# Routed experts: rows weighed on ScalarE and summed in memory by accumulating indirect transfers

## The chip, the core and the metric

One core of a Trainium2 chip (trn2) runs the whole program. The metric is the device time of one execution in microseconds. Engines: PE is TensorE, DVE VectorE, ACT ScalarE, POOL GpSimd, SP SyncE. Everything is fp32 unless a type is named.

## The reference

Two transformer blocks on 512 tokens of 1024 values. The change touches only the last stage, a mixture of experts in which each token goes to 4 of 32 experts:

```
logits = hf @ w_router + b_router
top_val, top_idx = top_k(logits, 4); gates = softmax(top_val)
# per expert e, over the tokens that chose it:
gu = xb @ w1[e] + b1[e]                       # 1024 -> 2048
gate, up = min(gu[:, :1024], 7), clip(gu[:, 1024:], -7, 7)
act = (up + 1) * gate * sigmoid(1.702 * gate)
y = (act @ w2[e] + b2[e]) * g[:, None]        # g: the pair's gate
out[tok] += y                                  # 4 addends per token
return rmsnorm(x + out, g_final)
```

Before it come a mixer, a first block with a product-key memory (512 gathers of rows of 8 KB) and a second block's attention and memory attention.

## The kernel before, in words

All engines' programs are written out by hand, in blocks; semaphores order them. The blocks before the experts take 1889 us. The middle part (`mid_sp`, L1301, loads its weights) ends with `store_rows`, which writes the normed token rows to `moe_dram` for the experts. `h` holds the residual, four tiles of 128 tokens.

*Positions.* Experts are sorted by their number of tokens; position p has a capacity of 128 rows (p 0 to 2), 96 (3 to 15, and 31) or 64 (the rest), by `capacity`. `ORDER` runs position 31 first, then alternates one of the wide positions with a 64-row one, then 15 and 30. A position has a first part of 64 rows and, if it is wider, a second part of 32 or 64 (`parts`). Tokens that are beyond the capacity would go to extra blocks of 64 rows, whose number is a register value (`each_extra`); the trace shows none.

*Weights.* An expert has six chunks of 2 MB (`expert_w`): four for gate and up, two for down. They go through a ring of nine slots. SP issues each load when PE has used the slot's last chunk (L2681, and L2710 for the last expert). Chunk number 8 lands on the tables from which the routing lists are made, so its load waits for `pe["slots2"]` and `dve["gk"]`.

*One expert.* POOL gathers its token rows (`rows_of`, L2725). PE transposes them (L2815), multiplies (gate and up: `into`, L2829; down: `out_of`, L2841; biases L2847), and transposes the activation (`transpose_act`, L2822). DVE clips (L3032), multiplies (L3037) and activates (`activate`, L3046 and L3048). ACT does sigmoid (L2965), copies (L2969) and, in `store` (L2974), copies the product from PSUM to `ysb`, which is the same memory as `usb`; then it issues the stores into `y_dram` (L2979), by position and row. `activate` writes `usb` again, so it first waits for the stores of the expert before (`y_st`). An fp32 product is four passes in the trace, so one call shows as four instructions.

*Routing lists.* During the first expert, DVE makes one-hot tables: `rowhot` (row in its position) and `poshot` (position), the same again for extra blocks. PE multiplies them into `slots` (L2805) and `slots2` (L2878), lists of the token in each row. Then DVE works out where each pair's row will lie in `y_dram` (`srow`, L3194 to L3203), the extra blocks' experts and the gates `gk` (L3204 to L3216).

*Fills.* Rows of `y_dram` that no expert writes are read by gathers all the same in some cases, so 37 stores fill them from SBUF during the middle part (L1360, L1366).

*End.* During the last expert POOL gathers, for each of 16 pairs (4 tiles by 4 choices), 128 rows from `y_dram` into weight slots that came free (`rows_back`, L2752), 12 at a time; DVE adds each to `h` times its gate (`add`, L3270). Two additions stand in DVE's order before the last expert's clip and three more before its activation. The rows of the last expert but one and of the last come in two rounds of four gathers (`add_late`, L3276). Then ACT squares and takes the root (L3013, L3016), DVE scales (L3284), SP stores.

Of the kernel before, what the change touches and what calls it, by code (L numbers as in the profile page):

```python
# [47 lines left out]
NBO = 32  # L48
BATCH = 32
# [17 lines left out]
for _name, _w in (("ident", P), ("lt", P), ("gt", P), ("ones", P), ("bones", P), ("wsmask", P),  # L67
                  ("iota", P), ("tok", NT), ("emod", P), ("rev", NE), ("rcount", 4 * PADU), ("zero", P), ("eps", 2)):
    _C[_name] = (_n, _w)
    _n += _w  # L70
# [13 lines left out]
def constants():  # L84
# [20 lines left out]
    put("eps", np.array([[EPS1, EPS2]]))  # L105
    return c
# [16 lines left out]
def build(nc, t, out):  # L123
    ctx = ExitStack()
    with ctx:
# [33 lines left out]
        y_dram = nc.dram_tensor("expert_rows", (OVER_AT + NBO * 64, D), F32).ap()  # L159


        last_dram = nc.dram_tensor("last_expert_rows", (64, D), F32).ap()
        prev_dram = nc.dram_tensor("last_but_one_expert_rows", (capacity(ORDER[-2]), D), F32).ap()
# [7 lines left out]
        rows_filled = sem("rows_filled")  # L171
# [1138 lines left out]
        def mid_sp(sp):  # L1310
# [17 lines left out]
            for j, unit in enumerate(unit_order):  # L1328
# [27 lines left out]
                if unit == ("o2", LAST, 3):  # L1356
                    fills = 0
                    any_rows = region(8192, 2 * D).rearrange("p (t d) -> p t d", t=2)
                    for i in range(OVER_AT, OVER_AT + NBO * 64, W):
                        sp.dma_start(y_dram[i:i + W, :].rearrange("(t p) d -> p t d", p=P), any_rows).then_inc(rows_filled, 16)  # L1360
                        fills += 1
                    by_position = y_dram[0:OVER_AT, :].rearrange("(q r) d -> r q d", r=P)
                    for cap, positions in ((64, range(16, NE - 1)), (96, list(range(3, 16)) + [NE - 1])):
                        for q in positions:
                            filled_from = 0 if q in ORDER[-2:] else cap
                            sp.dma_start(by_position[filled_from:P, q, :], any_rows[0:P - filled_from, q % 2, :]).then_inc(rows_filled, 16)  # L1366
                            fills += 1
# [10 lines left out]
            sp.wait_ge(rows_filled, 16 * fills)  # L1378
# [1160 lines left out]
        srow = small(16, NPAIR, I32)  # L2539
# [6 lines left out]
        lastm, rowf, lpart, glast, gk_rest, either = (small(1920 + i * NPAIR, NPAIR) for i in range(6))  # L2546
        erow = small(1920 + 6 * NPAIR, NPAIR, I32)
        prevm = small(227, NPAIR)
        lsum = small(243, NT)
        gl = [small(247 + i * NT, NT) for i in range(2)]  # L2550
        lrow = [small(255 + i * NT, NT, I32) for i in range(2)]
# [3 lines left out]
        before_last = sb("before_last", [P, 2], I32)  # L2555
        hot2 = sb("hot2", [3 * NE, 64], BF16)
        curs = sb("curs", [64, 1], I32)

# [9 lines left out]
        PIECE = NC // 2  # L2568

# [7 lines left out]
        def stored_rest(upto):  # L2577
            return sum(16 * P // x[1][1] for x in parts[0:upto] if len(x) > 1)

# [3 lines left out]
        pool_turn = sem("pool_turn")  # L2583
        x_t = sem("x_t")
# [13 lines left out]
        y_st = [sem(f"y_st{i}") for i in range(2)]  # L2598
        pe_turn = sem("pe_turn")

# [13 lines left out]
        NOWHERE = 2 * OVER_AT  # L2614
        Y_ROWS = OVER_AT + NBO * 64
        assert capacity(LAST_AT) == 64
        got = [slot(placed(FINAL - 1, c))[:, j * D:(j + 1) * D] for c in (3, 4, 5) for j in range(4)]
        late = [slot(placed(FINAL, 0))[:, j * D:(j + 1) * D] for j in range(NT)]
        prev = [slot(placed(FINAL, 2))[:, j * D:(j + 1) * D] for j in range(NT)]
        result = [slot(placed(FINAL, 1))[:, j * D:(j + 1) * D] for j in range(NT)]  # L2620
        NGOT = len(got)
        got_in = [sem(f"got_in{j}") for j in range(NGOT)]
        late_rows_in = [sem(f"late_rows_in{j}") for j in range(NT)]
        prev_rows_in = [sem(f"prev_rows_in{j}") for j in range(NT)]
# [8 lines left out]
        dvl += ["selr", "rsel", "selp", "psel", ("cap1", 0), ("cap2", 0), ("cap3", 0), ("cap4", 0), "beyond", "lastm", "prevm", "rowa", "rowhot", "poseq", "poshot"]  # L2633
        dvl += ["slots"]
        dvl += [("cap1", 1), ("cap2", 1), ("cap3", 1), ("cap4", 1), "spare", "spare64", "oge", "nb2", "bend2", "bst2", "live2", "any2", "turned2", "turn2", "stored2", "selb", "b2sel", "r2",
                "r64", "qge", "q2", "row2", "blk2s", "rowhot2", "blkeq", "blkhot2", "slots2", "base1", "base2", "gap", "gap2", "frow", "srow",
                "cmpb", "blk2f", "blk2m", "blk2", "esum", "erec", "gk", "rowf", "either", "erow", "grest", "gk_rest"]
        dvl += [(x, i) for i in range(2) for x in ("lpart", "lsum", "lrow", "glast", "gl")]
        dv = steps("dve", dvl)
        ac = steps("act", ["exp"])  # L2640
        BEFORE_CLIP, BEFORE_ACT = 2, 5
        end_dv = steps("dve", [("add", tt, k) for tt in range(NT) for k in range(EK)] + [("prev", tt) for tt in range(NT)]
                       + [x for tt in range(NT) for x in [("last", tt)] + ([("rstd", tt - 1), ("scale", tt - 1)] if tt else [])]
                       + [("rstd", NT - 1), ("scale", NT - 1)])
# [3 lines left out]
        pe = steps("pe", ["lgT", "lg", "cnt", "rank", "slots0", "slots", "slots2"])  # L2648
# [17 lines left out]
        with nc.Block() as block:  # L2666
            @block.sync
            def _(sp):
                def load(s, c, e6):
# [36 lines left out]
                for c in range(6):  # L2706
# [13 lines left out]
            def _(eng):  # L2720
# [14 lines left out]
                eng.wait_ge(dve_done, dv["slots2"])  # L2735

                def body(b):
# [7 lines left out]
                       .then_inc(rows_in, 16)  # L2745
                n = each_extra(eng, body)
# [3 lines left out]

                def rows_back(dst, src, nrows, index, sem_):
                    eng.indirect_dma_start(dst, None, src, bass.IndirectOffsetOnAxis(ap=index, axis=0),  # L2752
                                           bounds_check=nrows - 1, oob_is_err=False)\
                       .then_inc(sem_, 16)

                eng.wait_ge(dve_done, dv["gl", 1])
                eng.wait_ge(y_st[1], stored_rest(FINAL - 1))
                eng.wait_ge(y_st[0], eng.value_load(before_last[0:1, 1:2], min_val=32 * (FINAL - 1), max_val=32 * (FINAL + NOVER)))
                eng.sem_inc(pool_turn, 1)
                for i in range(NPAIR):  # L2760
                    if i < NGOT and i % 4 == 0:
                        eng.wait_ge(w_used[3 + i // 4], FINAL)
# [597 lines left out]
```

## Time and profile before

| | us |
|---|---|
| median of 3 runs (2967.68 to 2970.21) | 2967.72 |
| profiled execution | 2963.5 |
| its span | 2961.7 |
| PE busy in the span | 2394.2 (81%) |
| DVE busy | 1403.1 (47%) |
| ACT busy | 867.5 (29%) |
| POOL busy | 736.2 (25%) |
| data moved | 1098.90 MB, 371 GB/s on average |

Busy shares are averages over stages with different limits; the chain of waits says what the end hung on. From 1906 us on the program is in its expert stage. DMA shares are shares of the time of all 16 engines. A matmul that waits in the queue is drawn longer than it works, so a busy share alone doesn't show that PE sets the pace.

### The profile page before, as it was taken

Reading aid. Unit: us, or ns where it says so; the run is one execution under the profiler, and the core shown is the slowest. Engines: PE = TensorE matmul, PEld = TensorE weight load, DVE = VectorE, ACT = ScalarE, POOL = GpSimd, SP = SyncE. Lnnn points to the kernel's source line nnn. Section 1 sums busy time; section 2 is a strip of 40 time slices with the busy share of each in tenths; the row PEclk is TensorE's granted clock in tenths of the full one; section 3 lists DMA queues with packets and bytes.
Section 4 is the critical chain, followed back from the end, with each engine's and each line's share of the span. In section 5 each row is a group of like instructions: output and inputs, shape, how many; then the busy total and the mean of one; then the engine's idle time right before and its main releaser. Section 6 shows DMA issues by size and latency. Waiting matters only on the chain. (4 is left out here: it accounts for less than half of the span.)

```text
span 2961.7 us, 35151 instructions
## 1 busy us (share of the span) xinstructions
PE 2394.2 (81%) x13231; PEld 1140.0 (38%) x13231; DVE 1403.1 (47%) x3100; ACT 867.5 (29%) x2616; POOL 736.2 (25%) x663
## 2 busy tenths in 40 slices
PE   8998896675435695566678998699999999999995
PEld 4444442242001362124345787433333333333332
DVE  3967776767778766654655433531111111111115
ACT  1133334544445546522632341101000101001001
POOL 0313444433444445542643011100000000000003
PEclk9999998786656897587888999899999999999998
DMA  4349999999999999999999667899999999999996
GB/s 180 112 150 377 410 398 393 421 415 418 418 420 391 408 412 399 409 411 415 414 421 410 265 235 218 320 386 407 420 414 405 420 414 405 413 421 406 414 415 261
DMA packets 151243, 1098.90 MB, mean 371 GB/s; under 512 B 19616, under 2 KB 27040, under 8 KB 51648
## 3 DMA queue, kind: packets, MB, share of 16 engines
q0 software_dynamic: 80384, 553.69, 46.0%
q1 hardware_dynamic: 62112, 531.15, 44.8%
q10 hardware_dynamic: 8576, 11.80, 1.1%
q8 instruction: 105, 1.72, 0.2%
q14 instruction: 66, 0.54, 0.0%
HBM read 1071.80 MB, written 31.59 MB: 373 GB/s over the span
## 5 line engine op out<-in xcount | busy, mean ns | idle before, releaser
L2428 PE MATMUL banks<-arena,spare 128*32 128x512 f32 (+1 forms) x2048 | 484.1, 787 | 419.1 <-ACT spare L2290 412.6
L2061 POOL DMA_INDIRECT arena<-in_expert_uv,picked x512 | 584.7, 1142 | 870.8 <-PE banks L2428 619.1
L2196 DVE SCALAR_TENSOR_TENSOR arena<-arena 128x1024 f32<-128x1024 f32 x384 | 472.9, 1234 | 345.7 <-DMA arena<-in_expert_uv,picked 345.2
L2829 PE MATMUL banks<-arena,aT 128*64 128x512 f32 (+1 forms) x4032 | 616.1, 506 | 22.4 <-DMA arena<-in_expert_w 17.7
L2829 PEld LDWEIGHTS banks<-arena,aT 128*64 128x64 f32 (+1 forms) x4032 | 215.7, 126 | 396.4 <-issue 352.2
L2428 PEld LDWEIGHTS banks<-arena,spare 128*32 128x32 f32 (+1 forms) x2048 | 84.1, 132 | 710.4 <-ACT spare L2290 581.1
L3032 DVE TENSOR_SCALAR aT<-banks 128x512 f32<-128x512 f32 (+1 forms) x49 | 30.0, 614 | 593.3 <-PE banks L2847 593.3
L2841 PE MATMUL banks<-arena,aT 128*64 128x512 f32 (+1 forms) x2016 | 304.5, 502 | 0.3 <-DMA arena<-in_expert_w 0.3
L2725 POOL DMA_INDIRECT picked<-moe_rows,extra x32 | 31.0, 969 | 962.2 <-PE banks L2815 902.8
L2275 ACT ACTIVATE spare<-spare 128x2 f32<-128x2 f32 x256 | 51.9, 203 | 654.7 <-DVE arena L2196 654.1
L2196 DVE SCALAR_TENSOR_TENSOR arena<-arena,extra 128x1024 f32<-128x1024 f32 x128 | 156.5, 1224 | 89.3 <-DMA arena<-in_expert_uv,picked 89.1
L2841 PEld LDWEIGHTS banks<-arena,aT 128*64 128x64 f32 (+1 forms) x2016 | 103.9, 125 | 167.1 <-issue 146.6
L2969 ACT ACTIVATE aT<-banks 128x256 f32<-128x256 f32 x84 | 31.9, 383 | 382.0 <-PE banks L2822 382.0
L1294 PE MATMUL banks<-arena,aT 128*128 128x256 f32 x576 | 137.2, 395 | 0.0
L3046 DVE TENSOR_SCALAR aT<-banks 128x256 f32<-128x256 f32 x84 | 35.3, 420 | 214.5 <-PE banks L2847 214.5
L2290 ACT ACTIVATE spare<-spare 128x32 f32<-128x32 f32 (+1 forms) x512 | 136.3, 313 | 0.0
L2283 ACT ACTIVATE spare<-spare,picked 128x1 f32<-128x1 f32 x512 | 122.9, 287 | 11.7
L1294 PEld LDWEIGHTS banks<-arena,aT 128*128 128x128 f32 x576 | 111.0, 197 | 37.7 <-issue 20.1
L2965 ACT ACTIVATE aT<-aT 128x512 f32<-128x512 f32 (+1 forms) x49 | 27.8, 569 | 327.2 <-DVE aT L3032 327.2
L2390 PE MATMUL banks<-aT,arena 128*128 128x128 f32 (+1 forms) x512 | 122.0, 387 | 0.0
L1296 PE MATMUL banks<-aT,arena 128*128 128x256 f32 x448 | 107.1, 395 | 0.4 <-DVE aT L1258 0.4
L551 PE MATMUL banks<-aT,arena 128*128 128x512 f32 x240 | 103.4, 593 | 1.6 <-PEq L317 1.6
(368 smaller groups left out, 2715.5 us busy)
## 6 DMA issues: line engine op xcount, KB each, us to landing
arena<-in_expert_w SPq DMA_DIRECT2D x192, 2048.0 KB, 34.4
arena<-in_mid_w SPq DMA_DIRECT2D x71, 1024.0 KB, 9.1
expert_rows<-aT ACTq DMA_DIRECT2D x66, 128.0 KB, 9.2
arena<-in_w_q SPq DMA_DIRECT2D x4, 2048.0 KB, 11.1
arena<-in_expert_uv,picked POOLq DMA_INDIRECT x512, 12.6
expert_rows<-arena SPq DMA_DIRECT2D x8, 1024.0 KB, 14.5
arena<-in_w_in SPq DMA_DIRECT2D x3, 2048.0 KB, 13.7
arena<-in_w_out SPq DMA_DIRECT2D x2, 2048.0 KB, 7.8
```

Of the source, the lines that this page charges most:

```text
L551: mm = nc.tensor.matmul(bank[:, j % 8, :], w[:, k, col:col + P], aT[:, k, :], start=k == 0, stop=k == KD - 1)
L1294: mm = nc.tensor.matmul(dst, src[:, k, j * P:(j + 1) * P], w[:, k, :], start=k == 0, stop=k == KD - 1)
L1296: mm = nc.tensor.matmul(dst, w[:, k, j * P:(j + 1) * P], src[:, k, :], start=k == 0, stop=k == KD - 1)
L2061: eng.indirect_dma_start(places[place_of[n]], None, uv_rows, bass.IndirectOffsetOnAxis(ap=eidx[:, n:n + 1], axis=0))\
L2196: nc.vector.scalar_tensor_tensor(out=u, in0=u, scalar=1.0, in1=token_rows(tt)[:, g, :], op0=ALU.mult, op1=ALU.mult, accum_out=dots[:, k:k ...
L2275: nc.scalar.activation(gelus[:, k:k + PAIR], dots[:, k:k + PAIR], ACT.Gelu_apprx_tanh).then_inc(gelu_done, 1)
L2283: nc.scalar.activation(acts[:, k + i:k + i + 1], gelus[:, k + i:k + i + 1], ACT.Copy, scale=gates[:, n + i:n + i + 1]).then_inc(acts_done, 1)
L2290: nc.scalar.activation(diag[:, (n + i) % NDIAG, 0:width], ident4 if tt else ident2, ACT.Copy, scale=acts[:, k + i:k + i + 1]).then_inc(dia ...
L2390: mm = nc.tensor.matmul(bank[:, 4 + i % 2, t0 * P:t1 * P], w[:, k, g % 4 * P:(g % 4 + 1) * P], aT[:, k, t0 * P:t1 * P], start=k == 0, stop ...
L2428: mm = nc.tensor.matmul(bank[lo:lo + width, sum_bank[tt] + half, :], diag[:, (n + g) % NDIAG, 0:width], places[place_of[n + g]][:, D + hal ...
L2829: mm = nc.tensor.matmul(bank[tile, b_, 0:width], xT[:, c % 2 * 4 + k, r0:r0 + nrows], w[:, k * D + lo:k * D + lo + width], start=c % 2 == ...
L2841: mm = nc.tensor.matmul(bank[tile, YB[i], 0:width], hv[:, kk % nj, kk // nj * nrows:(kk // nj + 1) * nrows], w[:, k * D + lo:k * D + lo + ...
```

## The change

The gate is applied on ACT and the sum over a token's four experts is formed in memory. `sum_dram` (512 + 128 rows) starts as a copy of `h`. Each part of an expert goes to it in one indirect transfer on POOL's queue that adds: 128 partitions, each half a row (64-row parts) or a quarter (32-row parts). Row lists for it (`dest`) and gates by row (`gain`) are made from the one-hot tables; unused rows get an address past 512, one each. At the end SP reads `sum_dram` back into `h`. The fills, `y_dram`, the gathers back and DVE's additions go. Transfers that add wait for one another between experts.

In the middle part, SP:

```diff
-                if unit == ("o2", LAST, 3):
-                    ... 37 fills of y_dram
             for s in range(PASSES):
                 store_rows(s)
-            sp.wait_ge(rows_filled, 16 * fills)
+                if s != TOGETHER[0]:
+                    for tt in range(NT - 1) if s < LAST else (NT - 1, NT):
+                        rows_ = h[:, tt % NT, :]
+                        sp.dma_start(sum_dram[tt * P:(tt + 1) * P, :], rows_).then_inc(sum_begun, 16)
             sp.wait_ge(moe_rows_out, 64)
```

In the expert stage, SP, then POOL:

```diff
                     if i == 8:
-                        sp.wait_ge(pe_done, pe["slots2"])
-                        sp.wait_ge(dve_done, dv["gk"])
+                        sp.wait_ge(pe_done, pe["gains"])
...
+                sp.wait_ge(all_added, 16)
+                for tt in range(NT):
+                    sp.dma_start(h[:, tt, :], sum_dram[tt * P:(tt + 1) * P, :]).then_inc(sum_in[tt], 16)
```

```diff
+                def add_rows(i, nrows, index, landed):
+                    width = D * nrows // P
+                    eng.indirect_dma_start(halves_of_sum if nrows == 64 else quarters_of_sum, bass.IndirectOffsetOnAxis(ap=index, axis=0),
+                                           ysb[i][:, 0:width], None, compute_op=ALU.add)\
+                       .then_inc(landed, 16)
+
+                def add_first(s):
+                    eng.wait_ge(y_out[0], s + 1)
+                    if s:
+                        eng.wait_ge(y_added[0], 16 * s)
+                    after(eng, y_added[1], 16 * seconds[s])
+                    add_rows(0, 64, dest[0][:, ORDER[s]:ORDER[s] + 1], y_added[0])
+
+                def add_second(s):
+                    if len(parts[s]) > 1:
+                        eng.wait_ge(y_out[1], seconds[s] + 1)
+                        add_rows(1, parts[s][1][1], dest[1][:, ORDER[s]:ORDER[s] + 1], y_added[1])
                 for s, p in enumerate(ORDER[0:FINAL]):
...
                     rows_of(p)
+                    if s == 2:
+                        eng.wait_ge(sum_begun, 16 * (NT + 1))
+                        eng.wait_ge(dve_done, dv["gain", 1, 1])
+                    if s >= 2:
+                        add_first(s - 2)
+                        add_second(s - 2)
...
-                eng.wait_ge(y_st[0], n * 32 + (32 * FINAL + 32))
-                for tt in range(NT):
-                    rows_back(late[tt], last_dram, 64, lrow[1][:, tt:tt + 1], late_rows_in[tt])
+                add_second(FINAL - 1)
+                eng.wait_ge(y_added[1], 16 * seconds[FINAL])
+                eng.wait_ge(y_out[0], n + (FINAL + 1))
+                add_rows(0, 64, dest[0][:, LAST_AT:LAST_AT + 1], all_added)
```

PE: `gain_lists` stands in expert 0 between the transposes of the second part's activation and the down-projection's second chunk; `spread_lists` stands at the head of expert 1.

```diff
+                def gain_lists():
+                    eng.wait_ge(dve_done, dv["pair", 1, 3])
+                    for c in range(NPAIR):
+                        nc.tensor.matmul(lists[:, 0:3 * NE], rowhot[:, c, :], pairs[0][:, c, 1:4, :], start=c == 0, stop=c == NPAIR - 1)
+                    ... the same for the extra blocks
+                def spread_lists():
+                    eng.wait_ge(dve_done, dv["tlo", 1])
+                    for i, (x, lo, nrows, width) in enumerate(((0, 0, 64, 2 * NE), (0, 64, 32, 2 * NE), (0, 64, 64, 2 * NE), (1, 0, 64, 2 * NE))):
+                        for n in range(P // nrows):
+                            ... one product of 64 columns, from ident and table
```

ACT:

```diff
-                def store(i, nrows, nth, row, into=y_dram):
+                def weigh(i, nrows, nth, by):
                     width = D * nrows // P
                     eng.wait_ge(y_done[i], nth)
-                    nc.scalar.activation(ysb[i][:, 0:width], bank[:, YB[i], 0:width], ACT.Copy).then_inc(y_out[i], 1)
-                    eng.wait_ge(y_out[i], nth)
-                    for n in range(P // nrows):
-                        ... eng.dma_start(dst, ysb[i][...]).then_inc(y_st[i], 16)
+                    nc.scalar.activation(ysb[i][:, 0:width], bank[:, YB[i], 0:width], ACT.Copy, scale=by).then_inc(y_out[i], 1)
```

DVE: `srow` and `last_picks` go. After the first expert's `copy_rows` stand `which_blocks` (the former L3204 to L3216), `pair_gains` (gates split in three fp16 parts, then six products of 128x512 with the one-hot tables), `slot_gains` and `slot_lists` (small operations). Four small operations on `table` stand ahead of the first activation. `activate` waits for `y_added[i]` where it waited for `y_st[i]`. At the end only the scaling is left:

```diff
-                for i in range(BEFORE_CLIP):
-                    add(i)
                 clip_gate(0, 64, n + (FINAL + 1))
                 gated(0, 64, n + (FINAL + 1))
-                for i in range(BEFORE_CLIP, BEFORE_ACT):
-                    add(i)
                 activate(...)
-                for i in range(BEFORE_ACT, NPAIR):
-                    add(i)
-                ... add_late for the last two experts
                 for tt in range(NT):
-                    ...
+                    scale(tt)
```

## Rows read from the trace of the kernel before

**Rows 1.** Windows: stretch, length, busy (instructions) by engine, PEclk, DMA share, GB/s

```profile
2700.00:2800.00 100.00, 99.48 (x784) 38.37 (x782) 13.13 (x29) 9.87 (x22) 2.87 (x3) 1.00 1.01 407
```

**Rows 2.** Chain of waits, 1959 to 2843 us: start, duration, what

```profile
1959.56 9.03 PE banks L2829 x64
...
2018.60 9.03 PE banks L2829 x64
...
2205.22 9.03 PE banks L2829 x64
...
2334.63 40.87 DMA arena<-in_expert_w
...
2842.19 9.03 PE banks L2829 x64
```

**Rows 3.** DMA queues and issues, 2000 to 2600 us: packets, MB, share; landing last

```profile
q1 hardware_dynamic: 16158, 235.38, 95.1%
q10 hardware_dynamic: 4704, 6.43, 2.9%
q0 software_dynamic: 1872, 5.09, 2.6%
...
expert_rows<-aT ACTq DMA_DIRECT2D x42, 128.0 KB, 9.2
```

**Rows 4.** PE's waits, 1750 to 1890 us: total us, times, longest

```profile
PE banks L1294 <- DMA arena<-in_mid_w: 0.4, 1, 0.4
```

**Rows 5.** Windows, end of the middle part

```profile
1880.00:1885.00 5.00, 2.25 (x11) 1.64 (x9) 1.14 (x3) 1.44 (x3) 0.00 (x0) 1.00 0.23 91
```

**Rows 6.** Timeline of the first expert: start, duration, what, [idle before]

```profile
1922.18 0.56 PE L2805 MATMUL banks<-arena 128*128 128x32 f16 x16
...
1932.29 0.69 DVE L3189 TENSOR_TENSOR arena<-arena,cst 128x512 f16<-128x512 f16 x1
...
1938.15 1.22 DVE L3204 TENSOR_TENSOR arena<-arena,cst 128x1024 f32<-128x1024 f32 x1
...
1940.76 3.65 PE L2841 MATMUL banks<-arena,aT 128*64 128x512 f32 x16
...
1942.12 0.34 SPq L2681 DMA_DIRECT2D arena<-in_expert_w  x1
```

**Rows 7.** Landings of L2681's loads issued 1888 to 1890, then at 1982.13

```profile
DMA to landing us min/median/max: 7.7/12.2/16.6
...
DMA to landing us min/median/max: 10.3/10.3/10.3
```

**Rows 8.** Chain of waits, 1975 to 2002 us

```profile
1979.84 0.22 PE banks L2847 x2
...
1998.12 0.44 DVE aT L3046
```

**Rows 9.** Timeline of the last expert and the tail

```profile
2921.59 0.38 PE L2847 MATMUL banks<-spare,hot 96*64 96x512 bf16 x1
...
2923.93 1.28 DVE L3270 SCALAR_TENSOR_TENSOR h<-arena,extra,h 128x1024 f32<-128x1024 f32 x1 [3.51 <-DMA arena<-expert_rows,extra]
...
2927.51 8.05 PE L2841 MATMUL banks<-arena,aT 128*64 128x512 f32 x32
...
2935.83 0.60 ACT L2974 ACTIVATE aT<-banks 128x512 f32<-128x512 f32 x1 [7.82 <-PE banks L2847]
...
2955.64 1.06 ACT L3013 ACTIVATE arena<-h 128x1024 f32<-128x1024 f32 x1 [1.11 <-DVE h L3276]
...
2957.35 1.28 DVE L3284 SCALAR_TENSOR_TENSOR arena<-h,stat,grow 128x1024 f32<-128x1024 f32 x1
```

**Rows 10.** DMA issues of the whole span: times, KB each, median us to landing

```profile
arena<-expert_rows,extra POOLq DMA_INDIRECT x16, 23.0
...
arena<-last_expert_rows,extra POOLq DMA_INDIRECT x4, 3.1
```

More of the change, by code:

```diff
@@ L105, in constants @@
     put("eps", np.array([[EPS1, EPS2]]))
+    put("row", p)
+    put("half", p // 64)
+    put("quarter", p // 32)
     return c
@@ L2538, in build @@
         gk = small(0, NPAIR)
-        srow = small(16, NPAIR, I32)
+        gsplit = [small(16 + i * NPAIR // 2, NPAIR // 2, F16) for i in range(2)] + [small(227, NPAIR // 2, F16)]
+        grest = small(235, NPAIR)
         posf = small(32, NE)
@@ L2545, in build @@
         slots2 = small(194, NBO + 1, I32, 64)
[L2546 to L2551, printed above, removed]
+        table = [small(1920, 2 * NE), small(1920 + 2 * NE, 2 * NE, rows_=64)]
+        dest, gain = ([small(lo + i * NE, NE, dt) for i in range(2)] for lo, dt in ((1408, I32), (1408 + 2 * NE, F32)))
+        dest2, gain2 = small(1408 + 4 * NE, NBO + 1, I32), small(1408 + 5 * NE + 1, NBO)
+        pairs = [grow[:, :].bitcast(F16).rearrange("p (c j e) -> p c j e", c=NPAIR, j=4),
+                 extra[:, 384:384 + D].bitcast(F16).rearrange("p (c j e) -> p c j e", c=NPAIR, j=4)]
         any2 = small(263, 1)
@@ L2583, in build @@
         pool_turn = sem("pool_turn")
+        dest_copied = sem("dest_copied")
+        gain_copied = sem("gain_copied")
+        all_added = sem("all_added")
+        sum_in = [sem(f"sum_in{i}") for i in range(NT)]
         x_t = sem("x_t")
@@ L2597, in build @@
         y_out = [sem(f"y_out{i}") for i in range(2)]
-        y_st = [sem(f"y_st{i}") for i in range(2)]
+        y_added = [sem(f"y_added{i}") for i in range(2)]
         pe_turn = sem("pe_turn")
+        act_turn = sem("act_turn")
         def slot(i):
@@ L2639, in build @@
+        dvl += [("pair", x, j) for x in range(2) for j in range(1, 4)]
+        dvl += [(name, x) for x in range(2) for name in ("filled", "row", "thi", "tmid", "tlo")]
+        dvl += [("dest", 0), ("gain", 0), ("dest2",), ("gain2",), ("dest", 1, 0), ("dest", 1, 1), ("gain", 1, 0), ("gain", 1, 1)]
         dv = steps("dve", dvl)
         ac = steps("act", ["exp"])
[L2641 to L2644, printed above, removed]
+        end_dv = steps("dve", [x for tt in range(NT) for x in (("rstd", tt), ("scale", tt))])
@@ L2901, in _ @@
                             transpose_act(1, q)
+                    if s == 0:
+                        after(eng, h_e[1], pieces[1])
+                        gain_lists()
                     eng.wait_ge(w_loaded[placed(s, 5)], loads(s, 5))
@@ L2991, in _, with block_of_64 @@
                             copy_act(1, q, pieces[s] + q + 1)
-                    for i, (r0, nrows) in enumerate(parts[s]):
-                        if s == FINAL - 1:
-                            store(i, nrows, nth[i], r0, prev_dram)
-                        else:
-                            store(i, nrows, nth[i], p * P + r0)
-                def block_of_64(before, row, into, more):
+                    if s == 0:
+                        eng.wait_ge(dve_done, dv["gain", 1, 1])
+                    for i, (_, nrows) in enumerate(parts[s]):
+                        weigh(i, nrows, nth[i], gain[i][:, p:p + 1])
+                def block_of_64(before, more):
                     sigmoid(0, 64, before + (FINAL + 1))
@@ new lines, in slot_lists, with destinations, gains @@
+                def slot_lists():
+                    eng.wait_ge(pe_done, pe["spread"])
+                    def destinations(out_, i, n, times, place):
+                        V(nc.vector.scalar_tensor_tensor(out=out_, in0=lists[:, i * 2 * NE + n.start:i * 2 * NE + n.stop], scalar=times,
+                                                         in1=const(place).to_broadcast([P, n.stop - n.start]), op0=ALU.mult, op1=ALU.add))
+                    def gains(out_, i, n):
+                        V(nc.vector.tensor_copy(out_, lists[:, (2 * i + 1) * NE + n.start:(2 * i + 1) * NE + n.stop]))
+                    destinations(dest[0], 0, slice(0, NE), 2.0, "half")
+                    gains(gain[0], 0, slice(0, NE))
+                    destinations(dest2[:, 1:NBO + 1], 3, slice(0, NBO), 2.0, "half")
+                    gains(gain2, 3, slice(0, NBO))
+                    wide = next(p for p in range(NE) if capacity(p) < P)
+                    destinations(dest[1][:, 0:wide], 2, slice(0, wide), 2.0, "half")
+                    destinations(dest[1][:, wide:NE], 1, slice(wide, NE), 4.0, "quarter")
+                    gains(gain[1][:, 0:wide], 2, slice(0, wide))
+                    gains(gain[1][:, wide:NE], 1, slice(wide, NE))
```

274 lines of the change are left out of this document (130 added, 144 removed).

## The prediction

> **What bounds the kernel now.** I first took the windows view of the expert stage (from about 1909 us to the end). Over 2700 to 2800 us TensorE is busy 99.48 of 100 us and the sixteen DMA engines are busy all the time, at 407 GB/s [rows 1]. Both look full, so the next question is which of them sets the pace. The chain of waits answers it. The same point of the loop (up-projection of a 96-row expert) stands at 1959.56 and at 2018.60 us, so an undisturbed pair of a 96-row and a 64-row expert takes 59.04 us. From 2018.60 to 2205.22 us two such pairs and one of 128 and 64 rows take 186.62 us, so the long pair takes 68.54 us. Between 1959.56 and 2842.19 us lie 11 short pairs and 3 long ones: 11 x 59.04 + 3 x 68.54 = 855.1 us of TensorE work. They took 882.6 us. The other 27.5 us are waits for expert weights, as in the piece at 2334.63 us, where the chain runs through a weight load for 40.87 us [rows 2]. TensorE alone would need 27.5 us less. The rate of the DMA engines sets the end of this stage, although TensorE shows 99%: a matmul that waits for a weight tile is drawn long.
>
> So every byte moved in this stage counts, and it is the price of bytes that I look for. From 2000 to 2600 us the weights (q1) take 95.1% of the engines' time, the stores of expert rows (q10) 2.9%, the indirect gathers of token rows (q0) 2.6% [rows 3].
>
> After the last expert's down-projection the trace shows a tail: 2935.83 us (its copy out of PSUM) to the span's end at 2961.7 us. The profiled run took 2963.5 us, 1.8 more than its span.
>
> **The change, part by part.**
>
> *Fills removed.* 37 stores issued between 1754 and 1805 us go. In that stretch and up to 1890 us TensorE waited for its middle weights 0.4 us in all [rows 4]; its other waits are on VectorE. The cover is TensorE's own work, and nothing is late behind them. Gain between 0 and 0.4 us: 0.
>
> *Sum rows begun.* SyncE now stores token rows of `h` before the block ends: three tiles of 512 KB ahead of the last `moe_rows` store, two more behind it, ahead of expert weights 3 to 5. The queue is nearly empty then (the engines are busy 23% of 1880 to 1885 us [rows 5]). The three (1.57 MB, 3.8 us at 412 GB/s) could hold the block's end by 0 to 3.8 us, two more issues on SyncE cost their own fractions. I take 0.7, near the low end because of that idle time. The last two (1 MB) go into a queue that is refilled only after the expert numbers are known: hidden.
>
> *Lists for gates and destinations.* This is inside expert 0. VectorE today computes from 1938.15 us on what becomes `which_blocks`, up to `gk`, after which SyncE issues the held load of weight chunk 8 at 1942.12 us. Now `pair_gains` follows: six dependent small operations (about 0.2 each, 1.3 us) and six of 128x512 at 0.69 us (4.1), so the pairs are ready at about 1947.0 us. TensorE stands at `gain_lists` in its order, ahead of the down-projection that today starts at 1940.76 us. Its 32 small matmuls, three times as wide as the 16 that take 0.56 us, cost 1.1 to 3.4, say 1.6 us: it resumes at about 1948.6. With 0.4 us of list operations in front of the activation, that is 8.3 us of delay. `spread_lists` at the start of expert 1 adds 10 fp32 products in four passes of 64 columns, 40 instructions; a 512-column one takes 228 ns, so the bounds are 0.06 to 0.23 each, 2.4 to 9 us; I take 3.7, since the columns are few. Together TensorE is 12.0 us late [rows 6].
>
> What of this reaches the end? Only what starves the DMA engines, since they are the bound. Chunk 8 and all loads that wait for a used slot are issued that much later. The load issued at 1982.13 us landed after 10.3 us, and the first of an empty queue after 7.7 [rows 7], so only 2.6 us of work was queued before it. Twelve us later issue leaves 12.0 - 2.6 = 9.4 us in which the engines idle. Bounds: 5 (if only chunk 8's hold counts) to 12.
>
> *Stores become accumulating transfers.* Each expert now sends all its capacity rows (unused ones to rows past 512). Capacities sum to 2688 rows; without the last three experts 2432 rows, 9.96 MB, fall where the engines bind. A store reads SBUF and writes memory. An accumulate must also read the destination row. The trace before has no such transfer. From below: it costs no more than the store it replaces, 0 us, or even less (a store takes 2.9% of 882.6 us = 25.6 us in all; half of that gone is -12). From above: four times a store, +77. I take one more load of the same bytes on top of the store, since reading rows is what is added: 9.96 MB at 412 GB/s, +24 us. By the gathers' own rate (5.09 MB in 2.6%, so 6.43 MB of stores would be 3.3%) it would be +29 [rows 3].
>
> The Trainium skill (DMA: Bandwidth & Descriptors, Rules for kernel authors) states that the accumulate reads its destination and writes it later, and that nothing holds the bytes in between, so each must wait for the semaphore of the one before. By that the second read is there and the sum keeps its +24; without it the sum would be 24 lower. No run here shows it yet.
>
> *The new waits.* On GpSimd `add_first` waits for the copy out of PSUM, for the expert before, and for its predecessor's second part; queued behind it is the gather of rows two experts on, which is needed only some 30 us later. On VectorE `activate` waits for `y_added`, and TensorE's transposes wait for it. From the end of the 96-row expert's first part at 1980.06 us to the next activation at 1998.12 us lie 18.1 us [rows 8]. Minus 0.6 for the weighing and 0.8 for GpSimd to start, a landing may take 16.7 us. Stores land in 9.2 us at the median [rows 3]. I take 12 to 15: covered, no cost.
>
> *ScalarE's weighing* is the same copy with a scale, 0.60 us: 0. Its DMA issues go; it was never late.
>
> *Last expert.* Today VectorE stands in an addition that waited for a gather until 2923.93 us and ended at 2925.2, while the up-projection's last matmul had ended at 2922.0 [rows 9]. These 3.1 us go, and about 1.0 more, since TensorE's down-projection ran slower after its idle time (32 matmuls in 8.05 us, against 16 in 3.65 [rows 6, 9]). Late next is nothing: the weights have landed. -4.1, bounds -5 to 0.
>
> *Tail.* New chain from the copy's start: weigh 0.6, GpSimd 0.8, one accumulate on an empty queue. The gathers there land in 3.1 us [rows 10]; half the bytes, but with a second access, 4.0. Then four loads of 512 KB: the first lands after 3.1 like those gathers of the same size, and ScalarE is late next: four tiles of square (1.06 + 0.19) and root (0.29) with one table load 1.28, 4 x 1.65 + 1.3 = 7.9, then reciprocal and scale 1.5, and from the end of the last scaling the 3.1 that the span has today. 0.6 + 0.8 + 4.0 + 3.1 + 7.9 + 1.5 + 3.1 = 21.0, against 25.9 from 2935.83 to 2961.7 [rows 9]: -4.9, bounds -8 to +1.
>
> By the fit that the skill gives (same page, Anatomy of one DMA: 2.0 us fixed plus bytes at 436 GB/s) this accumulate of 256 KB would land in 2.6 us and the sum would be 1.4 lower.
>
> **Sum:** 0.7 + 9.4 + 24 - 4.1 - 4.9 = +25.1, so 2963.5 + 25.1 = 2988.6 us by the profiled execution. The median of the runs is 4.2 above that execution, so I forecast 2992.8, say 2993 us.
>
> **Rivals.**
> A. *Accumulate priced as a store.* If the second access overlaps the first, +24 becomes 0: sum +1.1, about 2969 us; a little cheaper than a store (-12) gives 2957. For it: the engines are held most by weights written into SBUF, and this traffic only reads SBUF. Against: stores do take time in proportion to their bytes. 0.22.
> B. *The DMA engines stop being the bound* (mechanism on the faster side): accumulates and the gone ACT queue leave the weights' stream so much room that TensorE never waits. Then the stage is 27.5 us shorter and pays the full 12.7 of start: -27.5 + 12.7 - 9.0 = -23.8, 2944 us. Against: stores take 25.6 us in all, so they would have to be nearly free. 0.06.
> C. *The landing holds VectorE* (slower side). It decides from 16.7 us of landing. The sixteen gathers at the end landed in 23.0 us at the median on the same queue [rows 10]. At 23, each turn from 96 to 64 rows loses 6.3 and the turn back 1.0: 15 x 7.3 = 110 us, TensorE bound: -27.5 + 12.7 + 110 - 9.0 = +86, 3054 us. 0.10.
> Forecast: 0.62.
>
> **How the numbers follow.** The forecast's own range is 2975 to 3015. 2955 to 3028 leaves out B, the far end of A and most of C: under 0.2. About 0.2% (5.9 us) is what a measurement can tell from no change: 2961.8 to 2973.6. Faster: B 0.06 and 0.08 of A with 0.02 of the forecast, 0.16. Same: 0.13 of A and 0.05 of the forecast, 0.18. Slower: 0.66.
>
> **What would show it.** Right: TensorE idle for some 6 us at about 1941 us and the loop 12 us late at 1960; q0 with far more engine time per MB than q10 had; longer DMA waits in the chain between 2200 and 2830 us; the pair still 59 us where it doesn't wait; tail about 21 us. Wrong: the distance from 1959.56 to 2842.19 unchanged or shorter (A, B); VectorE L3046 waiting for DMA in each pair (C); an accumulate that lands in over 6 us on an empty queue.

## The result, and the profile after

| us | before | after |
|---|---|---|
| median of the runs beside each other (5 and 5) | 2967.68 | 2994.32 (2989.43 to 3003.95) |
| ratio, 95% interval | | 1.0097 (1.0082 to 1.0112) |
| profiled execution, span | 2963.5, 2961.7 | 3003.95, 3002.0 |

The change makes the kernel slower by 26.6 us at the medians (24 to 33 us by the interval of the ratio). The forecast was 2993. The profiled execution of the kernel after is the slowest of its runs, and it was already 7.7 us late at the start of the middle part, in code that the change doesn't touch. So I compare distances between fixed points of each trace, not its times: from the first router product to the first up-projection of expert 1 (start), on to that of expert 29 (loop), on to the last copy out of PSUM (end), and to the end of the span (tail).

| us | start | loop | end | tail | sum |
|---|---|---|---|---|---|
| before | 70.7 | 882.6 | 93.6 | 25.9 | 1072.8 |
| after | 83.9 | 907.8 | 90.8 | 22.1 | 1104.7 |
| difference | +13.2 | +25.2 | -2.8 | -3.7 | +31.9 |

Three kernels that have the same code up to expert 29 (after, and two of the experiments) take 991.8, 988.6 and 987.2 us for start and loop together, so one profile can't tell 2 us of it.

The page after, part 1 and the end of part 3. There are fewer bytes than before (1098.90 MB), and yet it takes longer.

```profile
PE 2400.9 (80%) x13283; PEld 1140.1 (38%) x13283; DVE 1379.6 (46%) x3086; ACT 872.2 (29%) x2616; POOL 794.6 (26%) x690
DMA packets 143643, 1080.42 MB, mean 360 GB/s; under 512 B 16528, under 2 KB 23952, under 8 KB 44048
HBM read 1061.31 MB, written 19.40 MB: 360 GB/s over the span
```

**The start.** The timeline of the kernel after, expert 0, the counterpart of [rows 6] (start, duration, engine, line; in brackets the idle time before it and what ended it). Lines 2858, 2870 and 2876 are the gate and up projections, the down-projection and the biases; 2844 and 2851 the transposes of token rows and of the activation; 3265 and 2822 `pair_gains` and `gain_lists`; 3079 the activation; 3010 and 2721 the weighing and the accumulate.

```profile
1948.24 3.65 PE L2870 MATMUL banks<-arena,aT 128*64 128x512 f32 x16
1953.68 1.90 DVE L3265 TENSOR_TENSOR grow<-arena,extra 128x512 f16<-128x512 f16 x3
1955.49 1.89 DVE L3265 TENSOR_TENSOR extra<-arena,extra 128x512 f16<-128x512 f16 x3
1957.53 1.44 PE L2822 MATMUL banks<-grow,arena 128*128 128x96 f16 x16 [5.27 <-DVE extra L3265]
1960.03 0.41 PEld L2870 LDWEIGHTS banks<-arena,aT 128*64 128x64 f32 x4
```

TensorE is idle for 5.27 us (some 6 forecast) and then works on the lists; its next down-projection stands at 1960.03, after one at 1948.24. Before, the two chunks followed each other without such a hole (3.96 us apart). The windows view of the same moment shows why this counts: columns are the busy time of PE, PEld, DVE, ACT and POOL, then the granted clock, the DMA share and GB/s. The first two rows are the kernel after, the other two the kernel before at the same distance from the router product.

```profile
1952.27:1957.27 5.00, 0.00 (x0) 0.00 (x0) 4.76 (x13) 0.39 (x1) 0.00 (x0) 0.85 0.17 39
1957.27:1962.27 5.00, 4.74 (x38) 3.49 (x40) 1.72 (x10) 0.00 (x0) 0.00 (x0) 0.50 0.28 52
```

```profile
1943.89:1948.89 5.00, 5.00 (x78) 2.48 (x76) 0.00 (x0) 0.98 (x2) 0.00 (x0) 1.00 0.95 374
1948.89:1953.89 5.00, 5.00 (x50) 1.84 (x46) 0.00 (x0) 0.00 (x0) 0.00 (x0) 1.00 0.98 400
```

The DMA engines move 39 and 52 GB/s where they moved 374 and 400. The granted clock also falls to 0.50, 1.2 GHz, after the engine's idle stretch. In the first 140 us after the router product the DMA engines idle for 15.0 us, 5.0 before: 10.0 more, where 9.4 was forecast. Four experiments with the same lists (`plain`, `skip`, `order`, `fills`) idle for 15.6, 15.0, 13.1 and 13.1 us, so this number is known to some 2 us.

**The loop.** The DMA queues of the kernel after from 2000 to 2600 us, the counterpart of [rows 3] (packets, MB, share of 16 engines; then issues and the median us to landing).

```profile
q1 hardware_dynamic: 15593, 227.06, 92.0%
q0 software_dynamic: 6050, 11.67, 8.8%
summed_rows<-aT,extra POOLq DMA_INDIRECT x29, 12.1
```

q0 now holds the gathers of token rows, 2.6% before, and the accumulates: 6.2% of the time for 6.6 MB, 5.7 us of all engines per MB. The stores that they replace took 2.9% for 6.43 MB, 2.7 us per MB. The weights get 92.0% where they had 95.1%. The chain of waits of the kernel after, the counterpart of [rows 2]:

```profile
1981.19 9.03 PE banks L2858 x64
...
2040.23 9.03 PE banks L2858 x64
...
2238.19 38.23 DMA arena<-in_expert_w
...
2829.23 45.38 DMA arena<-in_expert_w
...
2889.03 9.03 PE banks L2858 x64
...
2913.01 0.48 ACT aT L3010
...
2913.76 14.64 DMA summed_rows<-aT,extra
...
2930.90 8.80 DMA picked<-moe_rows,extra
```

Where it doesn't wait, a pair still takes 59.04 us (2040.23 - 1981.19). So the 25 us of the loop are waits for weights and no work. The waits of TensorE and of VectorE (us in total, times, longest) say the same, and rule rival C out: VectorE's line 3079 waits for TensorE, never for an accumulate. The first row is the kernel before; between the same points of the kernel after the waits for weights are twice as long. The last row of TensorE holds two waits for gathers of token rows. The one of 8.9 us is that of the first expert, which took 8.0 before; the other, 4.3 us, was in no forecast.

```profile
PE banks L2829 <- DMA arena<-in_expert_w: 17.7, 9, 3.8
```

```profile
PE banks L2858 <- DMA arena<-in_expert_w: 36.2, 18, 3.4
PE banks L2844 <- DMA picked<-moe_rows,extra: 13.2, 2, 8.9
```

```profile
DVE aT L3079 <- PE banks L2876: 234.8, 47, 10.6
```

**The end.** The timeline of the kernel after around that 4.3 us wait, GpSimd and then TensorE:

```profile
2913.76 1.55 POOL L2721 DMA_INDIRECT summed_rows<-aT,extra  x1 [1.93 <-ACT aT L3010]
2928.45 0.19 POOL L2752 COPY extra<-extra 128x1 int32<-128x1 int32 x1 [13.15 <-DMA summed_rows<-aT,extra]
2930.90 1.02 POOL L2715 DMA_INDIRECT picked<-moe_rows,extra  x1 [2.26 <-issue]
...
2939.74 0.69 PE L2844 MATMUL banks<-cst,picked 64*128 64x64 f32 x4 [4.33 <-DMA picked<-moe_rows,extra]
...
2942.21 5.34 PE L2870 MATMUL banks<-arena,aT 128*64 128x512 f32 x16
```

GpSimd waits 13.15 us for an accumulate to land, to protect the order of the sums, and the gather of the last expert's token rows stands behind that wait in its queue. TensorE's transposes of these rows (L2844) wait 4.33 us for it, and the products behind them are slower: sixteen take 5.34 us, where 3.65 is usual (the granted clock is 0.50 during the transposes and 0.68 during the sixteen products). In the tail, the last accumulate (2982.30 us) lands after 4.9 us, and ScalarE's first square starts at 2990.45.

### The profile page after: what moved, and what is told of

It reads as the page before. It is cut to its first block and busy times, and to the rows that moved or that the text cites. A ratio compares the mean times of both kernels' runs of the same rounds, so it can differ in the third digit from the quotient of the medians.

```text
span 3002.0 us, 35101 instructions
## 1 busy us (share of the span) xinstructions
PE 2400.9 (80%) x13283; PEld 1140.1 (38%) x13283; DVE 1379.6 (46%) x3086; ACT 872.2 (29%) x2616; POOL 794.6 (26%) x690
## 3 DMA queue, kind: packets, MB, share of 16 engines
HBM read 1061.31 MB, written 19.40 MB: 360 GB/s over the span
## 5 line engine op out<-in xcount | busy, mean ns | idle before, releaser
L2721 POOL DMA_INDIRECT summed_rows<-aT,extra x49 | 76.7, 1565 | 328.0 <-ACT aT L3010 301.6
L1297 PEld LDWEIGHTS banks<-arena,aT 128*128 128x128 f32 x576 | 111.6, 198 | 38.0 <-issue 20.1
```

The source lines that it names most:

```text
L1297: mm = nc.tensor.matmul(dst, src[:, k, j * P:(j + 1) * P], w[:, k, :], start=k == 0, stop=k == KD - 1)
L2721: eng.indirect_dma_start(halves_of_sum if nrows == 64 else quarters_of_sum, bass.IndirectOffsetOnAxis(ap=index, axis=0), ysb[i][:, 0:width ...
```

## Experiments

The edits are against the kernel after, unless said otherwise. Ratios are to the kernel before, run beside each experiment on the same chip: in 5 rounds for `best`, `turn`, `best_mid` and `best_early`, in 3 for the others. The chips differ from one group of experiments to the next (the medians of the kernel before are 2963.3 to 2967.7 us), so compare ratios and distances, not the times themselves. "Sum" is the last column of the table above.

**plain.** Is it the adding that costs, or the transfer? The transfer writes over its rows, so the sum isn't formed.

```diff
-    ysb[i][:, 0:width], None, compute_op=ALU.add)\
+    ysb[i][:, 0:width], None)\
```

> The changed kernel with the same indirect transfers on the same queue, but plain stores without the addition (the sum is not formed, so its result is wrong at will; all waits stay). Theory: what the accumulate costs is its second access, the read of the destination rows, in engine time. Then q0's share between 2000 and 2600 us falls from 8.8% to 5.5%, the distance from expert 1's up-projection to expert 29's (907.8 us) falls by 25 to 30, and the time by about 27, to 2967 us. Rival: the engine time comes from the indirect path and its small packets, not from the addition: share and distance stay, 2994 us.

2959.51 us, ratio 0.9988 (0.9979 to 0.9998). Loop 881.9, end 83.9, tail 19.1, sum 1068.7: 36.0 below the kernel after. Its queues:

```profile
q0 software_dynamic: 3936, 11.65, 5.3%
...
summed_rows<-aT,extra POOLq DMA_INDIRECT x28, 7.1
```

The same bytes take 3.5% of the engines' time less and land 5 us sooner. The loop is 25.9 us shorter, which is all that the change had added to it (25.2). What remains of the transfers' engine time, 2.7%, is about what the stores took (2.9%). Rival A (the second access costs nothing) falls. The same bytes show as fewer, larger packets here (3936 against 6050 in q0), but small packets aren't the reason: in the kernel after an accumulate's packet of 2 KB takes 181 ns on average, and a store's packet of 2 KB in the kernel before took 85. That the extra time is the read of the destination isn't shown: the page counts 1061.31 MB read from HBM in both kernels. The end is 6.9 us and the tail 3.0 us shorter as well, which wasn't expected: GpSimd's wait at the end is 6.7 us instead of 13.15.

**narrow.** The same number of accumulates with an eighth or a quarter of the bytes each (64 columns; the rest of the rows isn't added).

```diff
-    halves_of_sum = ...("r (c d) -> (r c) d", c=2)
-    quarters_of_sum = ...("r (c d) -> (r c) d", c=4)
+    both with c=16
-    ysb[i][:, 0:width], None, compute_op=ALU.add)\
+    ysb[i][:, 0:64], None, compute_op=ALU.add)\
```

> The changed kernel with accumulating transfers of 64 values per partition instead of 512 or 256 (the rest of the sum is left out); their number, partitions, waits and queue stay. Theory (bytes on the DMA engines): q0 falls to 3 to 4.5% between 2000 and 2600 us, the distance between expert 1 and expert 29 falls from 907.8 by 38 or more, to 855 to 870, TensorE's own floor being 855; time about 2950 us. Rival (waiting for landings or the number of transfers holds the loop): the distance stays above 895.

2952.58 us, ratio 0.9963 (0.9954 to 0.9973). Loop 869.0, q0 4.3%. The end stays at 90.7 us. So the loop's cost goes mainly by bytes (a seventh of them takes 1.7% of the engines' time, where all took 6.2%) and the end's by the wait: the small accumulates still land in 10.9 us at the median, and GpSimd still waits 12.0 us for one at the end.

**skip.** Rows that no token fills are dropped instead of added past row 512.

```diff
-    ysb[i][:, 0:width], None, compute_op=ALU.add)\
+    ysb[i][:, 0:width], None, bounds_check=S * P // nrows - 1, oob_is_err=False, compute_op=ALU.add)\
```

> The changed kernel, but unused capacity rows (640 of 2688, 24%) are skipped by a bound on the destination index, as the gathers already do. If engine time goes by rows that move: 24% of 6.3% of 883 us = 13 us less, about 2981 us. Rival: a skipped descriptor costs as much as a moved one: 2994 us.

2983.22 us, ratio 1.0067 (1.0050 to 1.0084). Loop 895.4, that is 12.5 less. Its queue:

```profile
q0 software_dynamic: 6048, 10.42, 7.6%
```

The dropped rows go on showing as packets (6048 against 6050), but neither as bytes nor as engine time. About half of what the loop had lost was spent on rows that nobody reads. In the kernel before, those rows were stored too.

**later.** The lists wait until TensorE has finished expert 0's down-projection; the second list stands behind the first weight chunk of expert 1.

```diff
-                    if s == 1:
-                        spread_lists()
...
+                        if s == 1 and c == 0:
+                            spread_lists()
...
-                    if s == 0:
-                        gain_lists()
...                     # both chunks of the down-projection
+                    if s == 0:
+                        gain_lists()
```

> The changed kernel with gain_lists behind the whole down-projection of expert 0 and spread_lists behind the first chunk of expert 1; the held load of chunk 8 still waits for gain_lists. TensorE then resumes about 8 us earlier. Theory (the start's delay counts only as far as it starves the DMA engines; my 9.4 us were 12.0 minus 2.6 of queued work): the hold of chunk 8 (5.7 us) stays, so the end comes 3 to 4 us earlier. Rival (TensorE's delay reaches the end in full): 8 us earlier.

2988.45 us, ratio 1.0085 (1.0067 to 1.0104). The start is 6.6 us shorter than the kernel after's (4.4 and 4.0 shorter than those of `order` and `fills`, 81.7 and 81.3), but start and loop together are only 2.8 below the mean of the three kernels with the original order (989.2), about their own scatter. The DMA engines' idle time in the first 140 us, 13.6, lies among the 13.1 to 15.6 of the kernels with the original order: chunk 8 is now issued 65.4 us after the router product instead of 63.3 (61.4 to 63.3 in the same-code kernels), since it waits for the lists. So what TensorE gained at the start didn't reach the end in full. What did reach it is within the noise, and even its sign isn't settled by these runs.

**order.** The wait that holds GpSimd moves behind the last expert's gather.

```diff
-                eng.wait_ge(y_added[1], 16 * seconds[FINAL - 1])
                 eng.tensor_copy(dest2[:, 0:1], ...)
                 ... the gather of the last expert's rows
+                    eng.wait_ge(y_added[1], 16 * seconds[FINAL - 1])
```

> The changed kernel with GpSimd's wait for the second part of expert 29's accumulate moved behind the gather of the last expert's rows. Theory: that gather was issued at 2930.90 us, 14.6 us of landing too late, which cost TensorE 4.3 us of idle time at 2939.74 and some 2 us of lower granted clock. Both go: the time from the last chunk-c=2 piece of expert 29 to the span's end falls by 5 to 7 us. Rival: the last expert's weights would have been late anyway: 0 to 1 us.

2986.08 us, ratio 1.0074 (1.0057 to 1.0091). The end is 83.87 us instead of 90.84: 7.0 less. GpSimd in this kernel:

```profile
2901.82 1.55 POOL L2721 DMA_INDIRECT summed_rows<-aT,extra  x1 [1.93 <-ACT aT L3010]
2903.42 0.19 POOL L2751 COPY extra<-extra 128x1 int32<-128x1 int32 x1
2905.94 1.02 POOL L2715 DMA_INDIRECT picked<-moe_rows,extra  x1 [2.33 <-issue]
```

The gather now follows the accumulate by 4.1 us, where it was 17.1. TensorE's transposes start right behind the product before them, and the sixteen products behind take 3.65 us again: 4.3 us of idle time and 2.6 of slower products (1.7 here, 0.9 in the transposes) make the 7.0. So the place of this wait costs 7.0 us.

**fills.** The 37 stores of the kernel before are put back in the middle part, into rows that nobody reads.

```diff
+                if unit == ("o2", LAST, 3):
+                    ... the 37 fills of the kernel before
+            sp.wait_ge(rows_filled, 16 * fills)
```

> The changed kernel with the 37 fill stores of the middle part put back (into rows that nothing reads). Theory: TensorE's own work covers them: 0 us (within 1), the stretch from 1750 us to the first router product unchanged at 147 us. Rival: they held weights of the middle part or the block's end: 3 us or more slower.

2990.83 us, ratio 1.0085 (1.0067 to 1.0102). The middle stretch takes 146.9 us with the fills, 147.1 without, 146.5 in the kernel before; the sum is 1102.0 and 1104.7. Removing them gave nothing.

**best.** skip, later and order together, and VectorE computes the extra blocks' table behind `pair_gains` instead of ahead of it, while TensorE makes the lists; chunk 8 waits for both.

> The changed kernel with unused rows skipped, lists later, GpSimd's wait moved, and the experts-of-blocks table computed while VectorE waits. Sum of the single expectations: 13 + 4 + 6 + 1 = 24 us less than the changed kernel, about 2970 us, which is the time of the kernel before (2967.7) within its spread. If skipped rows cost as much as moved ones: 2983 us.

2972.44 us, ratio 1.0028 (1.0018 to 1.0038): still slower than before. Start 74.5, loop 898.7, end 83.9, tail 22.4, 1079.5 in all. The loop still has 16 us more than before: q0 takes 7.5% of the engines' time from 2000 to 2600 us, where stores and gathers took 5.5% before.

**turn.** In the kernel before, VectorE adds one gathered tile less ahead of the last activation. That is the edit that asks whether the forecast's two gains at the end are two.

```diff
-        BEFORE_CLIP, BEFORE_ACT = 2, 5
+        BEFORE_CLIP, BEFORE_ACT = 2, 4
```

> The kernel before with one addition moved from before the last expert's activation to after it (BEFORE_ACT 4 instead of 5). My forecast took 3.1 + 1.0 us for this wait. If it was on the path alone: TensorE's last product 3 to 4 us earlier and the end 3 to 4 us earlier. Rival: VectorE's row of additions to 2941.5 us ends as late as before and takes its place: the end moves by 1 us or less.

2964.53 us, ratio 0.9998 (0.9988 to 1.0007). The end is 2.5 shorter and the tail 2.7 longer. VectorE's timeline in this kernel:

```profile
2923.00 16.17 DVE L3270 SCALAR_TENSOR_TENSOR h<-arena,extra,h 128x1024 f32<-128x1024 f32 x12
2939.09 7.29 DVE L3276 SCALAR_TENSOR_TENSOR h<-arena,extra,h 128x1024 f32<-128x1024 f32 x6
```

VectorE adds without a pause from 2923 us on. The addition only changed its place. In the kernel before one bound, VectorE's additions, set the end; whoever takes the wait away and leaves the additions wins nothing.

**Three orders of the experts.** Position 15, a 96-row expert, stands last but one in `ORDER`, behind another, so that two 96-row experts stand in a row at the end. Does `best` gain by having it elsewhere? `best_mid` and `best_early` are `best` with this line, `before_mid` is the kernel before with it.

```diff
-ORDER.insert(NE - 2, 15)
+ORDER.insert(15, 15)     # best_mid, and before_mid (the kernel before)
+ORDER.insert(5, 15)      # best_early
```

> The version with all four repairs, and position 15 (a 96-row expert) moved from the end of the order to its middle (place 15 instead of 30). Near the end three experts in a row give the DMA engines time that nothing uses now that the gathers back are gone: the last weight chunk is in some 6 to 9 us before its use, while TensorE waits for weights earlier in the loop. Theory (the DMA engines bind until that slack): a wide expert in the middle turns the slack into fewer waits, 5 to 8 us less than the 2972.4 of the four repairs, about 2966 us, level with the kernel before. Rival: waits move to the end, 0 us.

> The same with position 15 at place 5, before the first waits for weights. The ring of nine slots limits how far loads may run ahead, and early on DMA engines and TensorE are level: 2 to 8 us less than the four repairs by the theory, 0 by the rival.

> The kernel before with position 15 at place 15. There the slack at the end carries the 16 gathers back. Theory: they now meet the last weights, TensorE waits at the end for what it no longer waits for in the middle, and the end does not move by more than 3 us; it may be up to 8 us later. Rival (the order alone is better for any kernel): 5 us faster.

best_mid 2968.56 us, ratio 1.0014 (1.0005 to 1.0023); best_early 2967.7, ratio 1.0001 (0.9992 to 1.0010); before_mid 2963.98, ratio 0.9996 (0.9986 to 1.0006). The order is worth some 4 us to `best` by the ratio (8 by best_early), and nothing to the kernel before. Between 5 and 8 were expected of best_mid. By the profiled executions, from the router product to the end of the span, the gain is smaller: 1079.5 us in `best`, 1076.6 in best_mid, 1077.6 in best_early, against 1072.8 and 1072.5 in the kernel before and before_mid. No version that forms the whole sum was faster than the kernel before. By the ratio best_early equals it, by this distance it is 4.8 us behind. Why the order helps only the new kernel wasn't taken apart.

## Why the prediction was right, and where it was not

The total is within 1.5 us of the measured median (2992.8 and 2994.3), and its direction, the bound and the main term held. That closeness is in part luck: two errors of opposite sign partly cancelled (5 and 6), the interval of the ratio leaves 24 to 33 us for the difference, and by the distances of the profiled executions it is 31.9 us, where the same terms of the forecast add up to 24.4.

1. *The DMA engines set the loop.* Right. The pair of 59.04 us is unchanged, and only waits for weights grew; `plain` and `narrow` move the loop by -26 and -39 us with no other edit than the kind or size of one transfer.
2. *Fills: 0.* Right (`fills`). *Sum rows begun: 0.7.* The middle stretch took 0.6 more than before. It takes 146.3 to 149.0 us in the ten kernels with the change (147.3 on average, `fills` and those without a whole sum among them) and 146.3 to 146.5 in the three without it, so 0.7 is possible and not shown.
3. *Lists: TensorE 12.0 late, 9.4 of it idle DMA engines.* TensorE was 13.2 late in the kernel after, 11.0 and 10.6 in `order` and `fills`. In the kernel after 3.1 had come up before the first down-projection: a first gather that landed 0.9 later, 1.6 of the first gate product (12.0 us against 10.4, at a granted clock of 0.75 against 0.87), and small waits. At `gain_lists` 7.8 followed (8.3 forecast), then 1.3 of a slower second chunk (granted clock 0.74), which was not forecast, and 1.0 at `spread_lists` (3.7). The forecast counted 40 instructions there; the trace has 20. The engines idled 10.0 more, 8 in `order` and `fills`. In `plain`, whose transfers cost what stores cost, start and loop together are 12.3 above before: that is what the lists cost in the end. 9.4 was 3 too small, though that is near the scatter of a profile. `later` speaks for the argument through the DMA engines: 4.0 to 6.6 us less for TensorE gave 2.8 or nothing.
4. *Accumulate: +24.* Measured 25.9 (`plain` against after, the loop). The adding costs time of the DMA engines that goes mainly by bytes, as forecast: it adds 3.0 us per MB (5.7 against 2.7), where a load's 2.4 was taken. That this time is a second access is what the forecast assumed; the traces show the time, not the read. By the engines' shares the addition is 3.5% of the time, some 31 us over the loop, and 26 of it reached the end.
5. *The new waits cost nothing.* Right for VectorE: the accumulates landed in 12.1 us at the median (forecast 12 to 15) with a budget of 16.7, and it never waited. Wrong for GpSimd, and this is the step that failed: "queued behind it is the gather of rows two experts on, which is needed only some 30 us later". That holds for every expert but the last. There the wait for the landing of expert 29's second part stands ahead of the gather that is needed next, and that cost 7.0 us (`order`); the forecast had put it at nothing. The chain of the code was read for the repeated case and not for the last turn of the loop.
6. *Last expert -4.1, tail -4.9.* The end and tail together are 13.5 us shorter than before once the wait is away (`order`: 83.87 + 22.13 against 119.5), 9.0 forecast. These 4.5 hid part of the other error. What I had not counted is a hole in TensorE's first product of the last expert in the kernel before, right behind the branch past the extra blocks, which the waits put down to "issue" (4.0 us, 3.7 in one piece at 2906 us, against 0.5 in the kernel after). It is gone where the gathers back are gone.

```profile
2901.84 0.64 PE L2829 MATMUL banks<-arena,aT 128*64 128x512 f32 x1 [0.29 <-issue]
2906.20 6.32 PE L2829 MATMUL banks<-arena,aT 128*64 128x512 f32 x22 [3.71 <-issue]
```

   What it waited for isn't shown. One trace of it: in both profiles with the hole, `before` and `turn`, a 16 KB packet of the instruction queue q8 starts inside it (2903.68 and 2902.56 us), and TensorE goes on 2.5 and 2.3 us later; in the kernel after and in `order` such a packet starts 6.1 and 3.5 us ahead of the same product. That would fit code that comes late behind the gathers, but no run tests it. Behind the hole the products are slower too (granted clock 0.76 from 2906.2 to 2912.0 us): the last expert's gate and up projections take 20.1 us, 14.4 in `order`. So the 9.8 by which `order`'s end is shorter than before are 3.7 of the hole, 2.0 of slower products behind it, 3.3 of the forecast's wait and 1.0 of its slower down-projection, less 0.2 at the branch. `turn` shows that -4.1 and -4.9 were not two gains of two causes: the additions were one bound.
7. *The tail's steps.* 22.1 measured, 21.0 forecast. GpSimd starts the accumulate 2.4 us after the weighing begins (1.4), it lands in 4.9 (4.0), the load back in 3.2 (3.1), and ScalarE's, VectorE's and the store's part takes 11.6 (12.5). In `plain` the same store lands in 2.7 us. By the fit of the Trainium skill (DMA: Bandwidth & Descriptors, Anatomy of one DMA) the estimate for 256 KB is 2.6 us: the trace agrees for the plain transfer (2.7) and not for the one that adds (4.9).

The sum as it came out, start to tail: 13.2 + 25.2 - 2.8 - 3.7 = 31.9 by the one profile, 26.6 by the medians. The three same-code kernels show that some 2.6 us of this difference of 5.3 are scatter of the profiled one. From the forecast's 24.4 (9.4 + 24 - 4.1 - 4.9) to 31.9 lead 2.9 more for the lists, 1.9 more for the accumulates, 7.0 for GpSimd's wait and 4.5 more gained at the end and tail: 31.7.

## What to carry to other kernels

Before a sum is moved from an engine into the DMA engines, see which of the two the end hangs on: here VectorE was 47% busy and had time, the DMA engines had none, and a transfer that adds took twice the engine time of a store (5.7 against 2.7 us per MB). When a new wait is put in an in-order queue, follow the queue through its first and its last turn too: here the repeated turn had room behind the wait and the last one hadn't. Send only the rows that are read: dropping the empty ones by the bounds check gave back half of what the loop had lost.

## What the runs showed of the hardware that I had not expected

- An accumulate's price beside a full stream is in the engines' time (5.7 us per MB against 2.5 for the plain indirect store in `plain`), and its latency is not much about bytes: 12.1 us with half rows and 10.9 with 256-byte pieces; the plain one 7.1.
- The instruction on GpSimd itself takes 1.56 us for an accumulate and 1.01 for the plain transfer of the same shape:

```profile
L2721 POOL DMA_INDIRECT summed_rows<-aT,extra x49: 1552/1562/1627, 1972.4 to 2982.3; - x49
```

```profile
L2721 POOL DMA_INDIRECT summed_rows<-aT,extra x49: 965/1006/1041, 1964.6 to 2940.8; - x49
```

(kernel after, then `plain`; ns at least, median, at most).
- Rows that the bounds check drops keep their packets in the trace (6048 against 6050) and lose their bytes and their time (10.42 against 11.67 MB, 7.6% against 8.8%).
- Small pieces are dear: in `narrow` the accumulates' 1.0 MB take 1.7% of 600 us, some 10 us per MB.
